# A two-layer block with 32 routed experts: single-pass slot products, smaller units, and one load of the largest expert's panels for its two units

## The reference

```python
logits = xt @ router_w + router_b
top_val, top_idx = lax.top_k(logits, 4);  gate = softmax(top_val)
# for each expert e, for its tokens:
gu = x @ w_gu[e] + b_gu[e];  g, up = gu[:, :1024], gu[:, 1024:]
g = minimum(g, 7);  up = clip(up, -7, 7)
y = ((up + 1) * (g * sigmoid(1.702 * g))) @ w_down[e] + b_down[e]
out[token] += gate * y
```

## Time and profile before

| | us |
|---|---|
| median of 3 runs (2965.52 to 2966.94) | 2966.05 |
| profiled execution | 2965.58 |
| its span in the trace | 2963.8 |
| TensorE busy | 2843.9 (96%) |
| VectorE busy | 1032.1 (35%) |
| ScalarE busy | 536.3 (18%) |
| mean granted TensorE clock | 0.975 |

### The profile page before, as it was taken

The page is one execution under the profiler, slowest core; times in us unless marked ns, Lnnn a source line. Parts: engine busy times, 40 slices in busy tenths (PEclk is TensorE's granted clock), DMA queues, the critical chain, the costliest instruction groups (busy, mean ns, idle before and its releaser), DMA issues.

```text
span 2963.8 us, 34847 instructions
## 1 busy us (share of the span) xinstructions
PE 2843.9 (96%) x14311; PEld 1395.7 (47%) x14312; DVE 1032.1 (35%) x1907; ACT 536.3 (18%) x1024; POOL 187.5 (6%) x282
## 2 busy tenths in 40 slices
PE   7999899999999999999969999998999999999999
PEld 3555544554444444444445545545545444444444
DVE  5941432333333333333253357244133222212101
ACT  3313310100001010001042233323133201000000
POOL 3210200000000000000000024000000000000000
PEclk9999899999999999999979999999999999999999
DMA  7256589999999999999963100200200141221310
GB/s 235 64 175 225 194 336 367 393 396 350 382 379 383 372 374 381 381 380 372 391 224 142 57 1 29 79 29 29 72 29 15 57 156 57 85 76 38 106 50 29
DMA packets 197405, 584.59 MB, mean 197 GB/s; under 512 B 15133, under 2 KB 23812, under 8 KB 197220
## 3 DMA queue, kind: packets, MB, share of 16 engines
q1 hardware_dynamic: 191744, 567.25, 50.8%
q0 software_dynamic: 4736, 14.88, 1.7%
q10 hardware_dynamic: 772, 0.26, 0.0%
HBM read 576.06 MB, written 4.19 MB: 196 GB/s over the span
## 4 chain that ended last, share of the span: by engine, by line
PE 89%; DVE 7%; ACT 1%; issue 1%; DMA 1%; SPq 0%; DVEq 0%; ACTq 0%; PEldq 0%
PE psum_all L213 86%; PE psum_all L221 3%; DVE scratch L1293 1%; DMA panels<-in_ada_w 1%; DVE scratch L3945 1%; DVE scratch L1350 1%; DVE hidden L2603 1%; SPq L190 0%; DVE panels L1293 0%; DVE resid L1755 0%; DVE scratch L1362 0%; DVE scratch L3344 0%; DVE panels L1350 0%; ACT hidden L458 0%; DVE hidden L1751 0%
## 5 line engine op out<-in xcount | busy, mean ns | idle before, releaser
L213 PE MATMUL psum_all<-panels,scratch 128*64 128x512 f32 (+4 forms) x6104 | 921.2, 479 | 4.8 <-issue 2.4
L213 PE MATMUL psum_all<-hidden,panels 128*128 128x512 f32 (+1 forms) x1792 | 788.3, 601 | 9.0 <-ACT hidden L458 8.7
L213 PEld LDWEIGHTS psum_all<-panels,scratch 128*64 128x64 f32 (+2 forms) x6104 | 363.8, 130 | 498.9 <-issue 432.8
L213 PEld LDWEIGHTS psum_all<-hidden,panels 128*128 128x128 f32 (+1 forms) x1792 | 333.2, 191 | 417.5 <-issue 402.4
L213 PE MATMUL psum_all<-scratch,panels 128*128 128x512 f32 (+2 forms) x816 | 306.8, 538 | 4.7 <-DVEq L4124 1.7
L213 PEld LDWEIGHTS psum_all<-scratch,panels 128*128 128x128 f32 (+1 forms) x816 | 152.1, 188 | 161.3 <-issue 149.4
L2603 DVE TENSOR_TENSOR hidden<-hidden,psum_all 128x512 f32<-128x512 f32 x264 | 164.4, 681 | 71.3 <-PE psum_all L213 70.9
L213 PE MATMUL psum_all<-scratch 128*64 128x128 f32 (+9 forms) x1284 | 161.9, 351 | 22.3 <-DVEq L3963 8.5
L213 PEld LDWEIGHTS psum_all<-scratch 128*64 128x64 f32 (+3 forms) x1284 | 109.0, 167 | 84.8 <-issue 60.5
L221 PE MATMUL psum_all<-const,scratch 128*128 128x128 f32 (+4 forms) x887 | 122.5, 269 | 17.9 <-DMA scratch<-in_c_ctx 7.7
L2311 ACT ACTIVATE scratch<-psum_all 128x512 f32<-128x512 f32 (+1 forms) x49 | 25.8, 527 | 602.0 <-PE psum_all L221 602.0
(11 more groups left out here) (356 smaller groups left out, 2085.4 us busy)
## 6 DMA issues: line engine op xcount, KB each, us to landing
panels<-in_exp_w_gu SPq DMA_DIRECT2D x132, 2048.0 KB, 13.4
panels<-in_exp_w_down SPq DMA_DIRECT2D x66, 2048.0 KB, 12.1
panels<-in_w_in SPq DMA_DIRECT2D x17, 2048.0 KB, 10.4
panels<-in_w_mod SPq DMA_DIRECT2D x11, 2048.0 KB, 8.2
panels<-in_ada_w SPq DMA_DIRECT2D x14, 1024.0 KB, 7.3
panels<-in_ada_w SPq DMA_DIRECT2D x5, 2048.0 KB, 20.8
panels<-in_ffn_w_gate SPq DMA_DIRECT2D x5, 2048.0 KB, 7.6
panels<-in_ffn_w_up SPq DMA_DIRECT2D x5, 2048.0 KB, 7.7
```

What stands on the lines that cost most here:

```text
L213: ins = self.pe.matmul(out, lhsT, rhs, start=start, stop=stop)
```

## The change

1. `expert_units` gives another list, still of 33: expert 0 gets 64 slots instead of 96; ranks 25 and 26 get 32 instead of 64. Four units have 128 slots, eleven 96, twelve 64 and six 32. The order begins with 64 (expert 0), 64 and 128 (both rank 0), 32, 32; then three times 128 + 32; then ten times 96 + 64; then 96 and 32.
2. Unit 2 (`SHARES`) uses the panels that unit 1 (`HOLDS`) loaded: unit 1 does not release them, unit 2 does not wait for them, and SyncE skips six loads. The loads up to unit 4 are written out ahead of the loop.
3. The slot matrices and the values are in the type of the single-pass products. The gate is cut in three parts that this type holds exactly (`dve_thirds`), so that a product has four columns, and VectorE adds the three with a small reduction.
4. `pe_share` of a 96-slot unit makes four tiles in a call instead of two, so that its 32-row products go four at a time, and waits for four free banks.
5. Buffers move to make room: `sel_last` to its own alias, `posr` onto a constant that is no longer used, the 32-slot bias operands get a third buffer.

```diff
-    large = [(NE - 1, 0, 96), (0, 0, S)] + [(r, 0, S if r < 4 else 96) for r in range(1, 15)]
-    less = [(0, S, HALF)] + [(r, 0, QUARTER) for r in range(27, 30)] + [(r, 0, HALF) for r in range(15, 27)] + [(30, 0, QUARTER)]
...
+    units = [(NE - 1, 0, HALF), (0, S, HALF), (0, 0, S), (25, 0, QUARTER), (26, 0, QUARTER)]
+    for i in range(3):
+        units += [(1 + i, 0, S), (27 + i, 0, QUARTER)]
+    for i in range(10):
+        units += [(4 + i, 0, 96), (15 + i, 0, HALF)]
+    return units + [(14, 0, 96), (30, 0, QUARTER)]
+
+HOLDS, SHARES = 1, 2
...
-RANK_CAPS = [(NE, 96), (NE - 1, -64), (27, 32), (15, 32), (4, 32), (1, 64)]
-UNIT_RANKS = [(0, 1, NE - 1, NE), (1, 2, 0, 1), (2, 31, 0, 15), (3, 8, 27, 30), (9, 32, 15, 27), (32, 33, 30, 31)]
+RANK_CAPS = [(NE, 64), (NE - 1, -32), (25, 32), (15, 32), (4, 32), (1, 64)]
+UNIT_RANKS = [(0, 1, NE - 1, NE), (1, 2, 0, 1), (2, 3, 0, 1), (3, 4, 25, 26), (4, 11, 26, 30), (5, 10, 1, 4),
+              (11, 32, 4, 15), (12, 31, 15, 25), (32, 33, 30, 31)]
...
@@ pe_slots
-            sels = [sel[:, u % 2, :, :], sel_last][:2 if UNITS[u][2] == 96 else 1]
+            sels = [sel_r[:, u % 2, :, :], sel_last][:2 if UNITS[u][2] == 96 else 1]
             for i, slots_at in enumerate(sels):
                 for t in range(TT):
-                    vals = gate_0[:, t, :] if u == 0 else gate_r[:, t, r:NE + 1:NE - r]
-                    ins = mm(bank[:, 2 * i:2 * i + 2], slots_at[:, t, :], vals, t == 0, t == TT - 1)
+                    vals = gate_0[:, t, :] if u == 0 else gate_r[:, t, r, :]
+                    ins = mm(bank[:, 4 * i:4 * i + 4], slots_at[:, t, :], vals, t == 0, t == TT - 1)
...
+        def dve_thirds(dve, step, dst, src, rest):
+            c = [dst[:, :, :, i] if len(dst.shape) == 4 else dst[:, :, i] for i in range(3)]
+            dve.tensor_copy(c[0], src).then_inc(dve_done, 1)
+            dve.wait_ge(dve_done, step.next())
+            dve.tensor_tensor(rest, src, c[0].bitcast(F32), ALU.subtract).then_inc(dve_done, 1)
+            dve.wait_ge(dve_done, step.next())
+            dve.tensor_copy(c[1], rest).then_inc(dve_done, 1)
+            dve.wait_ge(dve_done, step.next())
+            dve.tensor_tensor(c[2], rest, c[1].bitcast(F32), ALU.subtract).then_inc(dve_done, 1)
+            dve.wait_ge(dve_done, step.next())
...
@@ dve_slots
-                dve.tensor_copy(slot_tok[:, u:u + 1], bank[:, 1:2])
-                dve.tensor_copy(slot_vals[:, u, 0:2], bank[:, 0:2]).then_inc(banks.free, 1)
+                dve.tensor_copy(slot_tok[:, u:u + 1], bank[:, 3:4])
+                dve.tensor_copy(slot_vals[:, u, 1:2], bank[:, 3:4])
+                dve.tensor_reduce(slot_vals[:, u, 0:1], bank[:, 0:3], AX_X, ALU.add).then_inc(banks.free, 1)
...
-        def pe_rows_panel(pe):
+        def pe_rows_panel(pe, u):
             s, w = panels.use(DT // 2, D)
-            pe.wait_ge(panels.loaded[s], panels.arrived(s))
+            if u != SHARES:
+                pe.wait_ge(panels.loaded[s], panels.arrived(s))
             return s, w
...
@@ pe_expert_in, pe_expert_out
-                    if n == HALF and k == 3:
+                    if n == HALF and k == 3 and u != HOLDS:
                         ins.then_inc(panels.used[s], 1)
...
@@ pe_share
+            if UNITS[u][2] == 96:
+                if i % 4:
+                    return
+                nos = [y_fill(u, chunks(u) + i + j) for j in range(4)]
+                pe.wait_ge(shares_free, nos[3])
+                for m in range(2):
+                    f = slice((2 * m + i // 4) * P, (2 * m + i // 4 + 1) * P)
+                    for ys in (y_hi, y_lo):
+                        for h, no in zip(halves, nos[2 * m:2 * m + 2]):
+                            mm(moe_y(no)[:, :], ys[h, f], tokens_r[h, 0, :], ys is y_hi, False)
+                f = slice(512 + i // 4 * P, 512 + (i // 4 + 1) * P)
+                strips = [(slice(q * QUARTER, (q + 1) * QUARTER), no) for q, no in zip((0, 2, 1, 3), nos)]
+                for h, no in strips:
+                    mm(moe_y(no)[:, :], y_hi[h, f], tokens_r[h, 1, :], False, False)
+                for h, no in strips:
+                    mm(moe_y(no)[:, :], y_lo[h, f], tokens_r[h, 1, :], False, True).then_inc(shares_full, 1)
+                return
...
@@ sp_moe
-            with sp.Fori(0, N_UNITS // 2) as turn_no:
+            into(gu(e1, 0))
+            into(expert_dram(a["exp_w_down"], e0))
+            into(gu(e1, 1))
+            panels.at_load += 2
+            into(expert_dram(a["exp_w_down"], e1))
+            panels.at_load += 2
+            into(gu(e3, 0))
+            panels.at_load += 2
+            into(gu(e3, 1))
+            into(gu(e4, 0))
+            into(expert_dram(a["exp_w_down"], e3))
+            into(gu(e4, 1))
+            with sp.Fori(0, N_UNITS // 2 - 2) as turn_no:
```

More of the change, by code:

```diff
@@ L299, in build @@
         slots = [panel_room[:, i * PANEL:(i + 1) * PANEL] for i in range(SLOTS)]
+        with ExitStack() as over:
+            over.enter_context(nc.sbuf_tensor("under_slots", [P, where["chunk_keep"][0]], F32))
+            sel_last = over.enter_context(nc.sbuf_tensor("last_slots_in_r", [P, TT, S], F32R))
         const = sb("const", [P, table.shape[1]])
@@ L307, in build @@
             sel = over.enter_context(nc.sbuf_tensor("slots_of_units", [P, 2, TT, S], F32))
+        with ExitStack() as over:
+            sel_r = over.enter_context(nc.sbuf_tensor("slots_in_r", [P, 2, TT, S], F32R))
         s5c = sb("s5_columns", [P, 32, S5_PAIRS])
@@ L1780, in build @@
         router_b = r_part(NE)
-        cand, posm, posr, perm = (r_part(TT, NE) for _ in range(4))
+        cand, posm, perm = (r_part(TT, NE) for _ in range(3))
+        posr = con("gla_mask").rearrange("p (t e) -> p t e", e=NE)
         chosen_0 = r_part(TT + 1, NE)
@@ L1787, in build @@
         rank_col = r_part(1)
-        gate_r, gate_0 = r_part(TT, NE + 1), r_part(TT, 2)
-        gate, posx = r_part(NE, TT), r_part(NE, TT)
+        gate, posx = (v.rearrange("p t e -> p (t e)").rearrange("p (e t) -> p e t", t=TT) for v in (perm, chosen))
         cmp_t = part(4096, EXTRAS, NE)
@@ L2343, in pe_expert_in @@
             if n == QUARTER:
-                pe_quarter_in(pe, mm, u, bias, [pe_rows_panel(pe) for _ in range(2)], 0)
+                pe_quarter_in(pe, mm, u, bias, [pe_rows_panel(pe, u) for _ in range(2)], 0)
                 mid()
@@ L2416, in pe_expert_out @@
             if n == QUARTER:
-                pair = [pe_rows_panel(pe) for _ in range(2)]
+                pair = [pe_rows_panel(pe, u) for _ in range(2)]
                 pe_quarter_out(pe, mm, u, pair, moe_act_t[:, 0:256].rearrange("p (b q s) -> p b q s", b=2, q=4), no)
@@ L2430, in pe_expert_out @@
                     ins.then_inc(shares_full, 1)
-                elif n == HALF:
+                elif n == HALF and u != HOLDS:
                     ins.then_inc(panels.used[s], 1)
@@ L2438, in pe_expert_out @@
                 pe_quarter_out(pe, mm, u, pair, t, no)
-            mm.done(panels.used[pair[1][0]])
+            if u != HOLDS:
+                mm.done(panels.used[pair[1][0]])
         def share_tile(u, i):
@@ L2469, in pe_share @@
                 return
+            halves = [slice(j * HALF, (j + 1) * HALF) for j in range(2)]
+            if UNITS[u][2] == 96:
+                if i % 4:
[14 more added lines that the diff above has]
+                return
             m = i // 2
-            last = 0 if UNITS[u][2] == 96 else 1
             pe.wait_ge(shares_free, nos[1])
             f = slice(m * P, (m + 1) * P)
-            halves = [slice(j * HALF, (j + 1) * HALF) for j in range(2)]
             for h, no in zip(halves, nos):
@@ L2477, in pe_share @@
             for h, no in zip(halves, nos):
[L2478 to L2488 removed]
+                mm(moe_y(no)[:, :], y_lo[h, f], tokens_r[h, 0, :], False, True).then_inc(shares_full, 1)
         def pe_moe(pe, mm):
```

62 lines of the change are left out of this document (25 added, 37 removed).

## The result

The changed kernel takes 2898.30 us (median of 4 runs, 2896.42 to 2900.43) against 2966.49 us (4 runs, 2965.52 to 2968.39) of the kernel before beside it: a ratio of 0.977, 95% interval 0.9753 to 0.9786. The forecast was 2901 us, the range 2885 to 2924. The profiled execution took 2896.42 us, its span is 2894.8 us; against the profiled execution of before, 2965.58, that is 69.2 us less.

The account below looks back on a forecast made before the run. The prediction took TensorE to bound the expert stage, with DMA 1 to 4 us per pair behind. Savings of 77.6 us less losses of 10 + 2 + 1 gave 64.6, so 2965.6 became 2901 us, range 2885 to 2924.

Parts of the forecast that it names:

- A: Slot products of units 2 to 32: one record per matmul instead of two, saving 18.4 us (0 to 36).
- B: Shares of 96-slot units: 32-row products four abreast, 3.8 us instead of 5.3 per unit, saving 16.4 us (14.7 to 18.7).
- F: Panels held for units 1 and 2: 31 us less DMA, yet TensorE loses 10 us to late panels around units 4 to 12.
- C: Unit 0 goes from 96 to 64 slots, saving 14.7 us in its matrix work, shares and transposition.
- D: Two experts go from 64 to 32 slots, saving 11.8 us each, 23.6 us.
- E: Before unit 0: shorter slot products and VectorE chain, tokens turned in one piece, saving 4.5 us (2 to 5).
- unit 3's adds: Unit 3's shares made twice in a row in front of VectorE's adds: a loss of 2 us.
- the tail: Stage's end, where a 32-slot unit follows and both share calls are adjacent: waiting for four free banks loses 1 us.
- 1, DMA becomes the bound: 96 + 64 pairs: the queue's dry slice stays, each pair saves 1.2 instead of 2.8 us; 2917 us, chance 0.17.
- 2, the records do not get cheaper: Slot products: each record's weight load takes twice a record's spacing, so their saving falls to 0; 2919 us, chance 0.08.
- 3, the clock: Panel waits between units 4 and 11 halve TensorE's clock; three 128 + 32 pairs cost 192 us more, 3093; chance 0.02.
- 4, extra blocks: Expert units too small, so extra blocks run; one block costs 74 us, giving 2975 us; chance 0.02.

Follow-up runs that it names:

- half loads: Changed kernel with every panel load from unit 3's gate to the stage's end bringing only half its rows (results not the reference's): 2894.82 us, ratio 0.9766.
- later turning: Changed kernel with the next unit's tokens turned between the halves of the down product, not right behind the slot product: 2903.45 us, ratio 0.9785.
- both: Changed kernel with tokens turned between the down product's halves and panel loads halved from unit 3 on (results not the reference's): 2894.58 us, ratio 0.9756.
- the shares in pairs: Changed kernel with the share products of 96-slot units as before, pairs of 32-row products instead of fours: 2915.20 us, ratio 0.9825.
- float32 products: Changed kernel with its slot products as float32 again, two records per matmul, all else kept: 2931.44 us, ratio 0.9881.

## Why the prediction was right

The mechanism held: TensorE bounds the stage, its work became shorter in the places named, and the queue took a part of it back around units 4 to 11. The sum was 64.6 us, measured 69.2 between the profiled executions and 68.2 between the medians. That the total is so near is in part luck, since the errors of the terms cancel: A gave 6.2 us less than forecast, while B gave 2.2 more and F took 4.4 less. The terms, by the rows of both kernels and the experiments:

| term | forecast | measured | from |
|---|---|---|---|
| A slot products | 18.4 | 12.2 | 11 x 0.9, five x 0.45 |
| B shares of 96 slots | 16.4 | 18.6 | 11 x (5.3 - 3.61); undone 16.0 |
| C unit 0 | 14.7 | 14.4 | 59.69 - (417.97 - 373.59) = 15.3, less 0.9 of A |
| D two experts | 23.6 | 22.2 | undone 14.0, less 3.4 of a slow stretch, and the 11.6 that it had cost |
| E the start | 4.5 | 3.7 | 23.0 before, 19.3 at the same granted clock |
| F panels late | -10 | -5.6 | waits of 3.56 and 2.07 |
| unit 3's adds | -2 | -2.6 | 507.05 |
| the tail | -1 | -0.7 | waits 6.9 us, before 6.2 |
| slow stretches in the stage | 0 | 1.8 | lost before 1.7, 1.7, 1.3 and 0.5; after twice 1.7 |

All but E come to 60.3 us, and the stage lost 62.0; 1.7 us of it are assigned to no term. E's 3.7, 1.3 of the granted clock ahead of the stage, 1.3 by which the route was earlier already ahead of its count product, and 0.9 of the rest make the 69.2.

The two terms of 1.3 are luck of one execution. From the count product to the first expert matmul the kernel before ran at a granted clock of 0.50, and so did three kernels of the experiments (half loads, later turning, both), at 19.29 us each; the traced execution of the changed kernel had 0.59 and took 18.03. The kernel before, the changed kernel, and the one with half loads:

```profile
356.83:379.86 23.03, 18.75 (x100) 13.96 (x101) 10.34 (x39) 6.27 (x14) 4.00 (x11) 0.50 0.53 197
355.56:373.59 18.03, 13.20 (x83) 9.07 (x83) 10.15 (x40) 5.78 (x12) 3.54 (x7) 0.59 0.46 159
357.04:376.33 19.29, 14.60 (x83) 10.29 (x83) 11.10 (x46) 5.88 (x12) 3.54 (x7) 0.50 0.50 186
```

**A is the term that was mis-sized.** The price of a record was right: 4 records take 0.37 us and 8 take 0.88 (779.84 to 780.72), against 1.78 before. (The estimate from the Trainium skill, "TensorE: Matmul & The Clock Gate", "LDWEIGHTS (loading the stationary operand)", was 0.43 per product of 4; the trace has it 0.06 cheaper.) What failed is "20 others 0.42". Where the unit before has 96 or 128 slots, TensorE turns the second piece of its activations, makes the slots, and then turns the next unit's tokens into the same PSUM bank, of which there is one. ScalarE must first have copied the turned activations out of it, and the old, longer product was the cover of this copy. First the kernel before, then the changed one, the same place of a pair:

```profile
823.53 0.95 PE L213 MATMUL psum_all<-scratch,slots_of_units 128*128 128x2 f32 x8
824.34 0.53 PE L221 MATMUL psum_all<-const,scratch 96*128 96x96 f32 x4
```

```profile
810.19 0.59 PE L217 MATMUL psum_all<-gates_in_r,slots_in_r 128*128 128x4 f32 x4
811.00 0.52 PE L225 MATMUL psum_all<-const,scratch 96*128 96x96 f32 x4 [0.22 <-ACT scratch L2333]
```

0.81 us in both. Likewise in a 128 + 32 pair: 0.95 us before (550.18 to 551.13), with no wait, and 1.03 after (550.33 to 551.36), with a wait of 0.44. The prediction did not ask what TensorE would wait for once the product was shorter: of 20 products five gain their 0.45 (they stand ahead of a copy that is long done, as 383.12 to 383.55). The kernels with a later turning show that taking the wait away gives 0.4 us in a 128 + 32 pair and nothing in a 96 + 64 pair, but in them the single-pass products do have their full price: 1.3 us a 96 + 64 pair against float32, as 0.91 + 0.42 had said.

**B** came out at its upper end: 826.12 to 827.92 is 1.80 us a call, so 3.61 a unit. (The Trainium skill's rule in "TensorEngine Tiling (Array Packing)", "Key Properties", that a change of mode drains the engine, had given the 3.6; the trace agrees in that fewer changes cost less, and shows no drain by itself.) My 3.8 stood between this and 3.96, which gave each group a quarter of the alternating eight's 1.32 us; grouped, it costs less than that quarter.

**C, D, E** held within 1.4 us each. Unit 2's gate begins at 417.97 (forecast 419), the first expert matmul at 373.59 (375.4); in the eight kernels with the same route it begins at 376.1 to 378.0, so that this point was not better than the forecast but luckier.

**F.** The points of the ledger held: unit 3's second up panel landed at 464.41 (464.9), the waits stand at units 4 and 11, and the queue's share stands at 1.03 between. The lateness at unit 11 is 2.07 us there after 3.56 at unit 4, together 5.6 where the ledger gave 7 and I took 10; what I had added for the 0.9 us gaps that might close up did not come. With the shares in pairs it was 5.33, all at unit 4. But the sum put at nothing what follows a wait: the granted clock fell behind both, 1.7 us each time. And one sentence of F is wrong, "without the shared panels it would be six panels, 31 us, worse": loaded twice, the stage is 2.5 us longer. The six loads fall in the stretch in which the queue is otherwise dry.

**The rivals.** 1, DMA becomes the bound: it did not, as the half loads show (65.7 with the queue at 0.6). But its reason was nearer than its chance: with less matrix work the pair is 65.3 us. Its "dry slice stays" is wrong, for loads now queue up and land at 19 us. 2, the records do not get cheaper: false, 0.9 us a unit. 3, the clock: the waits do bring it to half, but for 3.4 us at a time and twice, which costs 3.4 us in all, less than the 5.2 in the stage before, and not for three pairs. 4, extra blocks: none ran. The panels' DMA queue moved 554.66 MB in the execution against 567.25 before, 12.6 less, which are the six panels left out; a block would have added as much.

## What to carry to other kernels

When small work that stands between another engine's copy and the instruction that waits for it gets shorter, subtract what it covered before counting the gain; here half a microsecond of small products hid a copy in 15 of 31 places. When an engine bounds a stage and the queue is within a few per cent of it, measure the queue's own floor by taking work out (here 65.3 us a pair) before planning the next saving on that engine. Loads that are left out at a point where no buffer comes free give almost nothing (here 2.5 us for 31 us of loads). And before an execution's total is credited to a term, look how far the same code's start and end scatter.

## What the runs showed of the hardware

- The granted clock fell to 0.50 for 3.4 us without any idle time, behind 16 records of four columns and 8 transpositions of 64 columns, 10 times behind 10 such runs in the kernel with float32 products, and cost 1.7 us each time. With 16 wide matmuls between the two kinds it did not fall behind any, and in the changed kernel, with 8 records in the run, neither. The kernel before has the same run with records of two columns, and the clock fell behind 2 of 11; at 1.00 it kept the same pair length, 68.38 us. So the run alone does not decide it; what else does is open. It makes the single-pass products worth more than their records: 30 us of the stage (1085.3 against 1055.2) instead of 12.2, of which 17 are ten slow stretches more.
- Twelve panels of 2 MB at 409 GB/s, 61.4 us, are not the whole price of a pair: gathers of 96 and 64 rows in place of 32 and 32 cost the queue 1.7 us where their bytes would be 0.96, and 2.2 us more are not explained.
- Small work inside a run of wide matmuls costs TensorE 0.1 to 0.2 us more than at its edge: the 64 matmuls that follow each other in 13.89 us (781.36 to 795.25) take 14.0 in two pieces, and with the tokens turned elsewhere the 0.22 us wait is gone and the pair is no shorter.
- A panel of 2 MB landed 7.6 us after its issue at best, and 18 to 20 us after it where six buffers kept the queue full, at the same 397 to 409 GB/s.
